# Sparse attention: the compressed branch's values from one block-diagonal table for a group's four heads

## What is computed

```
k_cmp, v_cmp = gelu(blocks @ w1) @ w2        # 15 rows of 128 for each of 4 groups
s     = einsum('bqghd,bngd->bghqn', q * scale, k_cmp)     # 4 heads of a group, 15 keys
p_cmp = masked_softmax(s, cmp_end <= t)
o_cmp = einsum('bghqn,bngd->bqghd', p_cmp, v_cmp)        # the step that is changed
y     = sum over branches of gate * o * silu(z)
```

## Time and profile before

| | before |
|---|---|
| median of 3 runs | 2006.16 us (2005.87 to 2006.3) |
| span of the profiled execution | 2003.7 us |
| the runs' median less that span | 2.5 us |
| TensorE busy | 1991.7 us, 99% |
| VectorE busy | 1317.6 us, 66% |
| ScalarE busy | 981.9 us, 49% |
| DMA, mean | 180 GB/s |

### The profile page before, as it was taken

The page is one execution under the profiler, slowest core; times in us unless marked ns, Lnnn a source line. Parts: engine busy times, 40 slices in busy tenths (PEclk is TensorE's granted clock), DMA queues, the critical chain, the costliest instruction groups (busy, mean ns, idle before and its releaser), DMA issues.

```text
span 2003.7 us, 30858 instructions
## 1 busy us (share of the span) xinstructions
PE 1991.7 (99%) x11849; PEld 1735.5 (87%) x11849; DVE 1317.6 (66%) x1931; ACT 981.9 (49%) x1444; POOL 73.8 (4%) x84
## 2 busy tenths in 40 slices
PE   9999999999999999999999999999999999999998
PEld 8998789988888888888999988888888888888887
DVE  7998877566666666578767766555555555555555
ACT  5664555354545454455456446544344434434443
POOL 2000132000000000100000001000000000000000
PEclk9999999999999999999999999999999999999999
DMA  9346578546464545756555555566666666666663
GB/s 293 96 152 234 164 214 250 165 131 189 126 195 131 182 145 169 247 154 199 169 168 148 155 171 191 178 189 190 194 188 190 193 191 189 189 195 181 196 192 107
DMA packets 203220, 360.74 MB, mean 180 GB/s; under 512 B 25393, under 2 KB 33937, under 8 KB 202449
## 3 DMA queue, kind: packets, MB, share of 16 engines
q1 hardware_dynamic: 200944, 351.82, 57.5%
q0 software_dynamic: 1664, 5.97, 0.9%
q10 hardware_dynamic: 480, 1.10, 0.1%
HBM read 355.96 MB, written 2.10 MB: 179 GB/s over the span
## 4 chain that ended last, share of the span: by engine, by line
PE 90%; DVE 7%; issue 1%; ACT 1%; DMA 0%; POOL 0%; POOLq 0%; DVEq 0%; ACTq 0%; SPq 0%
PE acc L529 36%; PE acc L533 10%; PE banks L563 9%; PE acc L563 9%; PE banks L529 8%; PE banks L566 4%; PE acc L566 4%; DVE w_high_low L1824 2%; PE banks L983 1%; PE acc L657 1%; PE banks L956 1%; PE acc L581 1%; PE acc L603 1%; PE banks L969 1%; PE banks L1035 1%
## 5 line engine op out<-in xcount | busy, mean ns | idle before, releaser
L1824 DVE TENSOR_TENSOR w_high_low<-raw,w_high_low 128x1024 fp32r<-128x1024 f32 x650 | 794.6, 1231 | 599.6 <-ACT w_high_low L1195 597.2
L1195 ACT ACTIVATE w_high_low<-raw 128x1024 fp32r<-128x1024 f32 x650 | 684.0, 1059 | 707.7 <-PE acc L529 292.9
L529 PE MATMUL acc<-w_high_low,x_high_low 128*128 128x512 f32 x1608 | 387.1, 396 | 0.4 <-DVE w_high_low L1824 0.4
L529 PEld LDWEIGHTS acc<-w_high_low,x_high_low 128*128 128x128 f32 x1608 | 299.5, 188 | 63.0 <-issue 0.8
L529 PE MATMUL acc<-w_high_low,h_high 128*128 128x512 f32 x1088 | 292.1, 390 | 0.1
L533 PE MATMUL acc<-x_high_low,w_high_low 128*128 128x256 f32 x2160 | 273.5, 285 | 0.0
L533 PEld LDWEIGHTS acc<-x_high_low,w_high_low 128*128 128x128 f32 x2160 | 263.4, 191 | 1.6
L563 PE MATMUL acc<-x_high_low,w_high_low 128*128 128x512 f32 x768 | 241.9, 396 | 0.4
L563 PE MATMUL banks<-x_high_low,w_high_low 128*128 128x512 f32 x768 | 241.2, 395 | 0.0
L529 PEld LDWEIGHTS acc<-w_high_low,h_high 128*128 128x128 f32 x1088 | 203.0, 188 | 41.8 <-issue 0.5
L566 PEld LDWEIGHTS banks<-x_high_low,w_high_low 128*128 128x128 f32 x768 | 144.3, 188 | 34.1
(11 more groups left out here) (388 smaller groups left out, 1643.5 us busy)
## 6 DMA issues: line engine op xcount, KB each, us to landing
raw<-in_b_w_in SPq DMA_DIRECT2D x128, 512.0 KB, 3.8
raw<-in_w_mlp_in SPq DMA_DIRECT2D x128, 512.0 KB, 3.7
raw<-in_w_mlp_out SPq DMA_DIRECT2D x128, 512.0 KB, 4.5
raw<-in_w_in SPq DMA_DIRECT2D x96, 512.0 KB, 4.0
raw<-in_kv_w SPq DMA_DIRECT2D x48, 512.0 KB, 4.2
raw<-in_a_w_in SPq DMA_DIRECT2D x32, 512.0 KB, 6.6
raw<-in_b_w_out SPq DMA_DIRECT2D x32, 512.0 KB, 4.7
raw<-in_w_out SPq DMA_DIRECT2D x32, 512.0 KB, 4.7
```

The costliest lines, as they stand in the source:

```text
L529: ins_ = nc.tensor.matmul(PAIRS[pair][:, t, :], xa[:, kt + j, t * P:(t + 1) * P], wa[:, k, j, :], start=first and n == 0, stop=last and n ...
L1195: nc.scalar.activation(WH[:, s % SPLIT, :, :], RAW[:, s, :, :], ACT.Copy).then_inc(hi_ready, WHOLE + 1 if first_one else 1)
L1824: V.tensor_tensor(WL[:, k, :, :], RAW[:, p % SLOTS, :, :], WH[:, k, :, :].bitcast(F32), ALU.subtract).then_inc(lo_ready, WHOLE + 1 if isin ...
```

## The change

The compressed values of the four heads come from one block-diagonal table instead of four separate products. CP shrinks to 16 columns a head, 64 in all. VectorE splits it into a rounded high part and the rest, side by side as 128 columns (CHL). `turn` transposes these 128 columns, `turned_probs` copies them with one activation, and `values` does two rounded matmuls of 512 columns. Their moving operand is VBD: row (part, head h, key k) holds the value row of key k in the 128 columns of head h and zero in the other heads' columns; the first matmul takes the rounded values, the second what rounding left of them (zero on the lower 64 partitions). ScalarE makes VBD for each group in step 3, with four activations whose scale is a 0/1 column from the constants. `turn` of n = 4 and 5 waits for the split (`cmp_split`), which VectorE does in step n + 1, after `outputs(n-1)` and before `maxima(n+1)`. Ahead of the attention the hidden rows are written eight times over (HCR), so that one matmul a group gives the values on all partitions, and VHL is made from them by a copy and a subtraction in place of VC's four copies.

```diff
-    VC = kv("v_cmp_rows", [P, KVH, HD])
+    VHL = kv("v_cmp_high_low", [P, 2, KVH, HD], F32R)
-    HS = comp("cmp_rows", [P, 2, P])
+    HCR = at("cmp_hidden_rows", [P, KVH, 8, 16], F32, placed["kv_sums"] + 12 * K1)
+    VBD = at("cmp_values_by_head", [P, 4, 2, HD], F32R, base + 124 * K1)
-    CP = nsa("cmp_probs", [P, 2, 4, 32])
+    CP = nsa("cmp_probs", [P, 2, 4, 16])
+    CHL = nsa("cmp_probs_high_low", [P, 2, 2, 64], F32R)
-    PTC = nsa("cmp_probs_cols", [P, 2, 4, P])
+    PTC = nsa("cmp_probs_cols", [P, 2, P], F32R)
 # TensorE, values ahead of the attention
+        pe.wait_ge(hidden_zeroed, 1)
         for h in range(KVH):
-            ins_ = nc.tensor.matmul(BK[1][0:NCMP, h * HD:(h + 1) * HD], HC[:, 1, 0:NCMP, h], W2[:, 1, :],
+            ins_ = nc.tensor.matmul(BK[1][:, h * HD:(h + 1) * HD], HCR[:, h, :, :].rearrange("p r n -> p (r n)"), W2[:, 1, :],
                                     start=True, stop=True)
 # TensorE, turn(n)
-                pe.wait_ge(p_ready, g * 10 + (n + 1))
                 if n:
                     pe.wait_ge(pt_ready, g * 10 + n)
                 if n in (4, 5):
-                    ins_ = nc.tensor.transpose(BK[2][:, 0:P], CP[:, n - 4, :, :].rearrange("p h n -> p (h n)"), ID)
+                    pe.wait_ge(cmp_split, g * 2 + (n - 3))
+                    ins_ = nc.tensor.transpose(BK[2][:, 0:P], CHL[:, n - 4, :, :].rearrange("p c n -> p (c n)").bitcast(F32), ID)
                 else:
+                    pe.wait_ge(p_ready, g * 10 + (n + 1))
 # TensorE, values(n)
-                    for h in range(4):
-                        ins_ = nc.tensor.matmul(BK[3][:, h * P:(h + 1) * P], PTC[:, n - 4, h, :],
-                                                VC[:, g:g + 1, :].rearrange("p o d -> p (o d)"), start=True, stop=True)
+                    pe.wait_ge(by_head, g + 1)
+                    for part_ in range(2):
+                        ins_ = nc.tensor.matmul(BK[3][:, :].rearrange("p (h d) -> p h d", h=4), PTC[:, n - 4, :], VBD[:, :, part_, :],
+                                                start=part_ == 0, stop=part_ == 1)
 # ScalarE, hidden rows
-            for i in range(2):
-                nc.scalar.activation(HC[:, i, 0:NCMP, :].rearrange("p n h -> p (n h)"), BK[2][:, 64 * i:64 * i + NCMP * KVH],
-                                     ACT.Gelu_apprx_tanh).then_inc(comp_act, 1)
+            nc.scalar.activation(HC[:, 0, 0:NCMP, :].rearrange("p n h -> p (n h)"), BK[2][:, 0:NCMP * KVH],
+                                 ACT.Gelu_apprx_tanh).then_inc(comp_act, 1)
+            copies = BK[2][:, 64:64 + NCMP * KVH].rearrange("p (n h) -> p h n", h=KVH).unsqueeze(2).to_broadcast([P, KVH, 8, NCMP])
+            nc.scalar.activation(HCR[:, :, :, 0:NCMP], copies, ACT.Gelu_apprx_tanh).then_inc(comp_act, 1)
 # ScalarE, turned_probs(n)
-                    for h in range(4):
-                        own = slice(32 * h, 32 * h + 32)
-                        ins_ = nc.scalar.activation(PTC[own, n - 4, h, :], BK[2][own, 0:P], ACT.Copy)
-                    ins_.then_inc(pt_ready, 1)
+                    nc.scalar.activation(PTC[:, n - 4, :], BK[2][:, 0:P], ACT.Copy).then_inc(pt_ready, 1)
+            def values_by_head():
+                act.wait_ge(comp_dve, 3)
+                for h in range(4):
+                    ins_ = nc.scalar.activation(VBD[:, h, :, :], VHL[:, :, bass.ds(g, 1), :].rearrange("p c o d -> p c (o d)"), ACT.Copy,
+                                                scale=const("own_head")[:, h:h + 1])
+                ins_.then_inc(by_head, 1)
 # ScalarE, step i, after turned_probs and probs
+                    if i == 3:
+                        values_by_head()
 # VectorE, ahead of the attention
-                steps.inc(V.memset(VC[:, :, :], 0.0))
+                steps.inc(V.memset(f32(VHL[64:P, 1, :, :]), 0.0))
+                V.memset(HCR[:, :, :, NCMP:16], 0.0).then_inc(hidden_zeroed, 1)
-                for r in range(4):
-                    ins_ = V.tensor_copy(VC[32 * r:32 * r + NCMP, :, :].rearrange("p h d -> p (h d)"), BK[1][0:NCMP, :])
...
+                steps.link(V.tensor_copy(VHL[:, 0, :, :].rearrange("p h d -> p (h d)"), BK[1][:, :]))
+                V.tensor_tensor(VHL[0:64, 1, :, :].rearrange("p h d -> p (h d)"), BK[1][0:64, :],
+                                f32(VHL[0:64, 0, :, :].rearrange("p h d -> p (h d)")), ALU.subtract).then_inc(comp_dve, 1)
-        steps.inc(V.memset(PTC[:, :, :, :], 0.0))
 # VectorE, in a group
+            def probs_split(n):
+                v.wait_ge(p_ready, g * 10 + (n + 1))
+                high_, low_ = (CHL[:, n - 4, part_, :].rearrange("p (h k) -> p h k", h=4) for part_ in range(2))
+                split(high_, low_, CP[:, n - 4, :, :], cmp_split)
                     if 2 <= i < 12:
                         outputs(i - 2)
+                    if i in (5, 6):
+                        probs_split(i - 1)
                     if i < 10:
                         maxima(i)
```

More of the change, by code:

```diff
@@ L45 @@
 PARAM_DMAS = 7
-GROUP_STEPS, QUARTER_STEPS = 62, 8
+GROUP_STEPS, QUARTER_STEPS = 64, 8
 U_AIN, U_GLU, U_AOUT, U_KV, U_NSA = 0, 4, 5, 7, 14
@@ L103 @@
 for _name, _width in [("ident", P), ("steps", 16), ("causal", 3 * P), ("strict", P), ("later", P), ("ones", P),
-                      ("cos", TOK), ("sin", TOK), ("cmp_bias", NT * 16), ("cmp_valid", NT * 16)]:
+                      ("cos", TOK), ("sin", TOK), ("cmp_bias", NT * 16), ("cmp_valid", NT * 16), ("own_head", 4)]:
     _CONST[_name] = (_at, _width)
@@ L139, in constants @@
     put("cmp_bias", np.where(valid, 0.0, NEG).astype(np.float32))
+    put("own_head", (row % 64 // 16 == np.arange(4)[None, :]).astype(np.float32))
     put("steps", np.broadcast_to(PH * np.concatenate([np.arange(8), 8 * np.arange(8)]).astype(np.float32), (P, 16)))
@@ L250, in build @@
     VW = kv("v_win_rows", [P, NT, COLS])
-    VC = kv("v_cmp_rows", [P, KVH, HD])
-    kv_end = (157 + 16) * K1 + 256 + 2048
+    VHL = kv("v_cmp_high_low", [P, 2, KVH, HD], F32R)
+    kv_end = (157 + 16) * K1 + 256 + 4096
     comp = region(kv_end, END)
@@ L351, in build @@
     comp_full, comp_act, comp_dve = sem("comp_full"), sem("comp_act"), sem("comp_dve")
+    hidden_zeroed, cmp_split, by_head = sem("hidden_zeroed"), sem("cmp_split"), sem("by_head")
     gate_split, gate_full, gate_tanh = sem("gate_split"), sem("gate_full"), sem("gate_tanh")
```

## The result

The changed kernel takes 2032.89 us (median of 4 runs, 2030.38 to 2036.25) against 2006.23 us before: ratio 1.0135, 95% interval 1.0122 to 1.0147. It is slower by 26.7 us where +17.9 was forecast. The direction and both waits are as forecast; the time lies 3.9 us above the range of 2014 to 2029. The profiled execution took 2032.46 us with a span of 2030.7, 27.0 above the span before.

The account below looks back on a forecast made before the run. TensorE, busy 1991.7 of 2003.7 us, was taken as the bound; first waits 13.6 plus net second waits 4.3 gave +17.9, a span of 2021.6, and with 2.5 us around it 2024 us; range 2014 to 2029.

Parts of the forecast that it names:

- both waits: TensorE waits for VectorE's split at turn(4) and turn(5) in each group: 13.6 us and net 4.3 us over four groups.
- the sum: First waits 13.6 us (lag + 2.69 us a group) plus net second waits 4.3 us: +17.9 us on the span, giving 2021.6.
- The second wait: At turn(5): late by another 1.48 us a group, net 1.08 after values(5) gives back 0.40; 4.3 us over four groups.
- The table at 1.6 us in the line of hand-overs: ScalarE's four step 3 activations head the ScalarE-VectorE chain before turn(4), moving its end by 1.6 us a group.
- The rival that hides it: Rival 2: the table's 1.6 us vanish in ScalarE's idle time, only split waits count; 2017.7 us, chance 0.15.
- The saving of 0.41 us a place: TensorE's values of n=4 and n=5: 2 matmuls replace 8, saving 0.41 us at 8 places, 3.3 us in all.
- the last one of the sum: Time taken by the row alone, TensorE's granted clock still 1.00 after the change: 2024 us.
- the third rival: Clock falls to 1.2 GHz after the long idle, one tick at half speed: 2.6 us a group, 2034.5 us, chance 0.08.
- the sign of this case: Listed as showing the forecast wrong: TensorE's ticks after the waits longer than 3.1 us.
- its own terms: Range around 2024: table 1.2 to 2.4 us (-1.6, +3.2), eight splits 0.3 to 0.7 us (-1.4, +1.8).
- Ahead of the groups: The table's inputs in the projection before: taken at 0, covered by the three tick lead; without it at most 0.5 us.

Follow-up runs that it names:

- the run with six matmuls: Changed kernel plus 6 unread 512-column matmuls before the wait at n=5 only, the idle time at n=4 left open; 2031.56 us.

## Why the prediction was wrong, and where it was right
- **The two waits**, their cause, place and order: right. Both stand at L971 with VectorE's subtraction as releaser, 8 times. Up to turn(4) the sum was 13.6 us and the trace has 13.7. The second wait was sized 0.8 us too low over the four groups, by the hand-over from values(4) to the outputs (0.11 taken, 0.47 and 0.23 measured in groups 0 and 1).
- **The table at 1.6 us in the line of hand-overs:** right, 1.70 us, and 1.6 us come off the line when it is moved to step 20. The rival that hides it fell.
- **The saving of 0.41 us a place:** right where the clock held (turn(5) to turn(6) -0.40 to -0.43). The two matmuls of values(5) are followed by turn(6) after 0.47 us, for 0.88 before.
- **The step that failed** is the last one of the sum, that the clock stays at 1.00 and that the ticks behind the waits take what they took. It stood among the rivals as the third, "the clock falls to 1.2 GHz after the long idle and one tick runs at half speed", priced at 10.5 us and given 0.08, against the argument that idle time and work alternate within few microseconds. The runs say: idle times of 2.85 to 2.87 us dropped it in 7 of 8 cases, those near 2 us in some, and 1.3 to 1.4 us in neither of two. A slow tick costs 1.6 us (4.59 for 3.00; where the low clock also caught the matmuls next to the tick, both together), not the 2.6 priced, which fits a clock that is back at 1.00 before the tick ends (430.0 in group 0). The five slow ticks make 7.9 us of the 9.1 that the profiled span lies above the sum; the rest is 0.8 of the second wait, 0.1 of the first, and the 0.3 ahead of the groups. That the third rival's 2034.5 comes within 1.6 us of the measured time is partly luck: four ticks at 2.6 us stand there for five at 1.6.
- **The range:** the prediction had named the sign of this case, ticks longer than 3.1 us, but its range left the case out. It also misadds its own terms: -1.6 -1.4 and +3.2 +1.8 around 2024 give 2021 to 2029, not 2020 to 2028; and from one group's turn(4) to the next's they give 4.8 us more, not about 4.5 (8.4 measured from group 0 to 1).
- **The Trainium skill's rule**, TensorE: Matmul & The Clock Gate, section "Loop structure matters more than you think", that idle time between matmuls can lower the clock, is what this trace shows (0.57 in the 4 us behind turn(4)). The prediction weighed it and took the row of the kernel before. That row could not decide it: in the stage no idle time of TensorE was longer than 0.3 us.
- **Ahead of the groups:** taken at 0; the +0.3 us of this profile are within the scatter named above, so nothing speaks against it.

## What to carry to other kernels
When a change puts a wait on the engine that is the bound, ask where the awaited work stands in its own engine's order: two VectorE instructions of 0.2 us each cost 23 us more behind the low part of a weight slice and the outputs than in front of them (2032.9 and 2010.0 us), with the table left where it was. Price an idle time of TensorE of 2 us and more with the clock that may fall behind it, even if the trace at hand shows only the upper level: in the trace of the kernel before, TensorE never waited longer than 1.2 us. Work on an engine that is busy half of the time is not free when it stands between two hand-overs: move it to a step in which nobody waits, which here was worth 6.3 us (2010.0 to 2003.7).

## What the runs showed of the hardware
TensorE's granted clock fell to its lower level right behind a single idle time of about 2 to 2.9 us, out of steady work at 1.00. It was still 1.00 during the idle time, fell in the work behind it (0.1 us after turn(4) began in group 1 of the changed kernel, 1.5 us after in group 1 of the run with the table in step 20), and was back about when the next tick ended. It doesn't fall every time. Over the profiles, in front of turn(4), it fell behind 7 of 8 idle times of 2.85 to 2.87 us (the one exception in group 1 of the run with six matmuls), 2 of 4 of 2.34 to 2.35, both of 1.98 and 1.99, and neither of 1.40 and 1.31. Behind the idle times of 1.74 to 2.10 us in front of turn(5) it fell in 2 of 12, both times when the tick behind turn(4) had been slow already. A kernel at this edge can be expected to have times that spread, and this one's did: 2030.4 to 2036.3 us over 4 runs, against 2005.9 to 2006.6 before. What decides between the cases stays open. Matmuls that nobody reads, in the idle time, kept the clock up and made the kernel 9 us faster.
